# SSD stage of a two-layer hybrid model: three units of the next group's input projection among the head pairs' y products, and the older out product of the last group after its own y

## What is computed

```python
proj = u @ w_in
z = proj[..., :SSD_D_INNER]
xbc = jax.nn.silu(dwconv_centred(proj[..., SSD_D_INNER:SSD_D_INNER + SSD_CONV_DIM], conv_w, conv_b))
...
y = y_fwd + y_bwd + xh * d_skip.reshape(SSD_GROUPS, SSD_HPG)[:, :, None]
y = y.reshape(bsz, seq, SSD_D_INNER) * jax.nn.silu(z.astype(jnp.float32))
yg = y.reshape(bsz, seq, SSD_GROUPS, SSD_D_INNER // SSD_GROUPS)
yg = yg * lax.rsqrt(jnp.mean(yg * yg, axis=-1, keepdims=True) + NORM_EPS)
y = yg.reshape(bsz, seq, SSD_D_INNER) * norm_w.astype(jnp.float32)
return (y @ w_out).astype(u.dtype)
```

## Time and profile before

| | us |
|---|---|
| median of three runs | 1836.24 |
| lowest and highest run | 1832.72, 1839.12 |
| the profiled execution: its time | 1833.54 |
| the profiled execution: its span | 1831.8 |
| TensorE busy (matmuls) | 1578.1 (86%) |
| VectorE busy | 1282.2 (70%) |
| ScalarE busy | 781.0 (43%) |
| y stage of group 0, about | 149 to 183 |
| y stages of groups 1, 2 and 3 | 274 to 312, 402 to 442, 532 to 572 |
| last out products of the SSD stage | 585 to 609 |

### The profile page before, as it was taken

The page is one execution under the profiler, slowest core; times in us unless marked ns, Lnnn a source line. Parts: engine busy times, 40 slices in busy tenths (PEclk is TensorE's granted clock), DMA queues, the critical chain, the costliest instruction groups (busy, mean ns, idle before and its releaser), DMA issues.

```text
span 1831.8 us, 20798 instructions
## 1 busy us (share of the span) xinstructions
PE 1578.1 (86%) x7275; PEld 1269.4 (69%) x7275; DVE 1282.2 (70%) x1673; ACT 781.0 (43%) x1323; POOL 165.6 (9%) x200
## 2 busy tenths in 40 slices
PE   3984987987985799999998777887898999999996
PEld 1753756755754588778877556887686888888875
DVE  4577766866875676696679898997466677663355
ACT  3348465473473455513442322221234555542242
POOL 1153000000000450000001020000010000000000
PEclk7987998998997899999999986675899999999998
DMA  2233313303320523252334564662232323333231
GB/s 71 82 92 117 92 46 115 105 33 118 112 70 23 114 87 97 81 184 92 102 133 161 191 240 143 162 166 53 66 104 70 102 92 100 95 97 104 90 94 64
DMA packets 189607, 190.57 MB, mean 104 GB/s; under 512 B 47566, under 2 KB 178206, under 8 KB 185438
## 3 DMA queue, kind: packets, MB, share of 16 engines
q1 hardware_dynamic: 168926, 187.52, 32.4%
q10 hardware_dynamic: 20608, 2.10, 0.9%
HBM read 165.27 MB, written 24.31 MB: 103 GB/s over the span
## 4 chain that ended last, share of the span: by engine, by line
PE 59%; DVE 25%; ACT 9%; issue 4%; DMA 2%; ACTq 1%; SPq 1%; DVEq 0%
PE ring L1829 19%; PE ring L1830 18%; PE ring L1831 18%; ACT rows L992 3%; ACT rows L1002 3%; DVE w_lo L1224 2%; DVE rb L1631 2%; DMA rows<-log_decays 1%; DVE ul L1238 1%; PE pe_y L1972 1%; DVE cc L1348 1%; DVE s_prod L1590 1%; DVE tab L1551 1%; DVE ytmp L1502 1%; DVE rstd L1247 1%
## 5 line engine op out<-in xcount | busy, mean ns | idle before, releaser
L879 ACT ACTIVATE w_hi<-w_raw 128x1024 fp32r<-128x1024 f32 (+1 forms) x233 | 239.9, 1029 | 656.7 <-PE ring L1831 626.2
L1829 PE MATMUL ring<-uh,w_hi 128*128 128x512 f32 (+1 forms) x1160 | 461.9, 398 | 36.5 <-DVE w_lo L1224 30.1
L1830 PE MATMUL ring<-ul,w_hi 128*128 128x512 f32 (+1 forms) x1160 | 455.7, 393 | 0.0
L1831 PE MATMUL ring<-uh,w_lo 128*128 128x512 f32 (+1 forms) x1160 | 455.0, 392 | 0.0
L1224 DVE TENSOR_TENSOR w_lo<-w_raw,w_hi 128x1024 fp32r<-128x1024 f32 (+1 forms) x233 | 278.0, 1195 | 188.4 <-ACT w_hi L879 188.2
L1829 PEld LDWEIGHTS ring<-uh,w_hi 128*128 128x128 f32 (+1 forms) x1160 | 220.1, 190 | 94.7 <-DVE w_lo L1224 25.7
L1830 PEld LDWEIGHTS ring<-ul,w_hi 128*128 128x128 f32 (+1 forms) x1160 | 220.1, 190 | 47.3 <-issue 2.1
L1831 PEld LDWEIGHTS ring<-uh,w_lo 128*128 128x128 f32 (+1 forms) x1160 | 219.7, 189 | 47.4 <-issue 0.6
L1829 PE MATMUL ring<-gh,w_hi 128*128 128x512 f32 x480 | 190.5, 397 | 29.2 <-DVE w_lo L1224 16.1
L1830 PE MATMUL ring<-gl,w_hi 128*128 128x512 f32 x480 | 189.1, 394 | 0.0
L1831 PE MATMUL ring<-gh,w_lo 128*128 128x512 f32 x480 | 189.0, 394 | 0.0
(11 more groups left out here) (250 smaller groups left out, 2173.9 us busy)
## 6 DMA issues: line engine op xcount, KB each, us to landing
w_raw<-in_ffn_w_up SPq DMA_DIRECT2D x88, 512.0 KB, 3.5
w_raw<-in_ffn_w_down SPq DMA_DIRECT2D x40, 512.0 KB, 3.5
w_raw<-in_ssd_w_in SPq DMA_DIRECT2D x32, 512.0 KB, 4.4
rows<-log_decays SPq DMA_DIRECT2D x16, 1024.0 KB, 5.9
s_tables<-tab SPq DMA_DIRECT2D x16, 1024.0 KB, 6.2
slot<-s_tables SPq DMA_DIRECT2D x16, 1024.0 KB, 7.4
w_raw<-in_ssd_w_out SPq DMA_DIRECT2D x16, 512.0 KB, 3.5
w_raw<-in_ple_w_gate SPq DMA_DIRECT2D x16, 512.0 KB, 3.5
```

Of the source, the lines that this page charges most:

```text
L879: act.activation(w_hi[u % 2][:, 0:n], w_raw[:, u % 2, 0:n], ACT.Copy).then_inc(hi_done, 1)
L1829: pe.matmul(o, wh[:, k, c], rh[:, k0 + k, :], start=first and k == 0, stop=False)
L1830: pe.matmul(o, wh[:, k, c], rl[:, k0 + k, :], start=False, stop=False)
L1831: mm_ = pe.matmul(o, wl[:, k, c], rh[:, k0 + k, :], start=False, stop=last and k == nk - 1)
```

## The change

The core of the diff (the tiles `yh_last` and `yl_last` are a second pair for the last group's normed y; they lie where `xd` and `car` lay, which are done with by then):

```diff
@@ sync
-                    for n in range(GT + 2):
+                    for n in range(GT + 1):
                         row_load(n)
+                    xbc_loads(1, 2, 3)
+                    row_load(GT + 1)
                 else:
-                    xbc_loads(g, 2, 6)
+                    xbc_loads(g, 3, 6)
...
-                        for n in range(2):
-                            xbc_loads(g + 1, n, n + 1)
-                            row_load(GT * g + GT + n)
+                        xbc_loads(g + 1, 0, 1)
+                        row_load(GT * g + GT)
+                        xbc_loads(g + 1, 1, 3)
+                        row_load(GT * g + GT + 1)
@@ scalar
-                    if hp + 1 < GT and g:
-                        hi_to(w + hp + 3)
+                    if g:
+                        if hp < (GT if g + 1 < GROUPS else 2):
+                            hi_to(w + hp + 3)
+                    elif hp == 3:
+                        hi_to(w + 2)
...
-                if g < GROUPS - 1:
-                    hi_to(U[("xbc", g + 1)] + 2)
-                if g:
+                if g + 1 < GROUPS:
+                    hi_to(U[("xbc", g + 1)] + 3)
+                if 0 < g < GROUPS - 1:
                     act.wait_ge(unit_done, w + 4)
...
+                if g + 1 == GROUPS:
+                    hi_to(w + 5)
@@ vector
+                ahead = U[("xbc", g + 1)] if g + 1 < GROUPS else None
                 for hp in range(GT):
                     weigh(hp)
-                    if g:
+                    if g and hp < 2:
                         lo_to(w + hp + 2)
                     add_yoff(hp)
                     if hp:
                         finish(hp - 1)
-                    if hp + 1 < GT and g:
+                    if g and (hp < 2 or hp == 2 and ahead):
                         take_out(g - 1, hp + 1)
+                    if ahead and hp:
+                        lo_to(ahead + hp - 1)
                 finish(GT - 1)
...
                 dve.tensor_scalar(var[:], pe_s[:], 1.0 / GC, EPS, ALU.mult, ALU.add).then_inc(gvar, 1)
+                if ahead:
+                    lo_to(ahead + 3)
                 dve.wait_ge(gstd, g + 1)
                 dve.reciprocal(ytmp[:], var[:]).then_inc(grstd, 1)
                 dve.wait_ge(grstd, g + 1)
-                if g < GROUPS - 1:
-                    lo_to(U[("xbc", g + 1)] + 2)
...
+                if not ahead:
+                    take_out(g - 1, 3)
+                    lo_to(w + 4)
...
+                if not ahead:
+                    lo_to(w + 5)
@@ tensor
                 u = U[("xbc", g)]
-                for i in range(3):
-                    for kg in range(2):
-                        product(u + 2 * i + kg, T[("xbc", g)] + 2 * i, 4, 4 * kg, uh0, ul0, first=kg == 0, last=kg == 1)
-                        if g and (i, kg) == (0, 0):
-                            group_square(g - 1, GT - 1)
+                for n in range(3 if g else 0, 6):
+                    xbc_product(g, n)
...
+                def meanwhile(out, xbc):
+                    if g and out:
+                        out_product(g - 1, out)
+                    if g + 1 < GROUPS and xbc is not None:
+                        xbc_product(g + 1, xbc)
+
                 transposes(0)
                 for hp in range(GT):
-                    if hp + 1 < GT and g:
-                        out_product(g - 1, hp + 1)
+                    meanwhile(*((1, None), (2, None), (3 if g + 1 < GROUPS else None, 0), (None, 1))[hp])
                     if hp + 1 < GT:
                         transposes(hp + 1)
                     outputs(hp)
-                    if hp:
-                        group_square(g, hp - 1)
-            group_square(GROUPS - 1, GT - 1)
+                if g + 1 < GROUPS:
+                    meanwhile(None, 2)
+                    group_square(g, GT - 1)
+                else:
+                    group_square(g, GT - 1)
+                    meanwhile(3, None)
```

More of the change, by code:

```diff
@@ L178, in bidir_hybrid_kernel @@
         zs = sb("zs", [P, GT, SEQ], where=ssd)
+        last_y = ExitStack()
+        yh_last = sb("yh_last", [P, GT, SEQ], F32R, last_y)
+        yl_last = sb("yl_last", [P, GT, SEQ], F32R, last_y)
+        last_y.close()
         xd = sb("xd", [P, 2, GC], where=ssd)
@@ L198, in bidir_hybrid_kernel @@
         ssd.close()
+        YH, YL = [yh] * (GROUPS - 1) + [yh_last], [yl] * (GROUPS - 1) + [yl_last]
         def ffn_memory(layer, where):
@@ L1029, in _ @@
                     act.wait_ge(yn_done, GT * g + m + 1)
-                    act.activation(yh[:, m, :], zs[:, m, :], ACT.Copy).then_inc(yh_done, 1)
+                    act.activation(YH[g][:, m, :], zs[:, m, :], ACT.Copy).then_inc(yh_done, 1)
+                if g + 1 == GROUPS:
+                    hi_to(w + 5)
             for i in range(4):
@@ L1509, in _ @@
                                              in1=ytmp[:], op0=ALU.mult, op1=ALU.mult).then_inc(yn_done, 1)
+                if not ahead:
+                    take_out(g - 1, 3)
+                    lo_to(w + 4)
                 for m in range(GT):
                     dve.wait_ge(yh_done, GT * g + m + 1)
-                    dve.tensor_tensor(yl[:, m, :], zs[:, m, :], yh[:, m, :].bitcast(F32), ALU.subtract
+                    dve.tensor_tensor(YL[g][:, m, :], zs[:, m, :], YH[g][:, m, :].bitcast(F32), ALU.subtract
                                       ).then_inc(yl_done, 1)
+                if not ahead:
+                    lo_to(w + 5)
             for i in range(4):
@@ L1903, in out_product, with xbc_product @@
                 def out_product(g, i):
-                    product(U[("out", g)] + i, T[("out", g, i)], GT, 0, yh, yl)
+                    product(U[("out", g)] + i, T[("out", g, i)], GT, 0, YH[g], YL[g])
+                def xbc_product(g, n):
+                    product(U[("xbc", g)] + n, T[("xbc", g)] + n // 2 * 2, 4, n % 2 * 4, uh0, ul0, first=n % 2 == 0,
+                            last=n % 2 == 1)
                 u = U[("xbc", g)]
-                for i in range(3):
-                    for kg in range(2):
-                        product(u + 2 * i + kg, T[("xbc", g)] + 2 * i, 4, 4 * kg, uh0, ul0, first=kg == 0, last=kg == 1)
-                        if g and (i, kg) == (0, 0):
-                            group_square(g - 1, GT - 1)
+                for n in range(3 if g else 0, 6):
+                    xbc_product(g, n)
                 z_product(0)
```

## The result

The changed kernel is slower: 1846.44 us median of ten runs (1841.52 to 1848.56) against 1837.58 us (1832.72 to 1839.12) for ten runs of the kernel before, measured beside it. The ratio is 1.0050, with a 95% interval of 1.0039 to 1.0060. The profiled execution took 1845.06 us with a span of 1843.3 us, 11.5 more than the span of before.

What follows compares the result with a forecast made beforehand. Bounds: log decays and ScalarE's decays in the y stage, VectorE's chain to X4's split in the convolution stretch. 0.7 + 2 x (1.7 + 0.8 + 2.0) - 5.2 = +4.5 us on 1836.24 gives 1840.7; range 1831 to 1847.

Steps and rivals of the forecast that it cites:

- second rival: Stops before X0 and X4 cost full clock price, 2.1 and 2.5 us: +8.6 in all, or 1845 us; chance 0.33.
- Nothing of the three units comes off the path: Convolution stretch: X4's split keeps its place and four units still follow, so moving three units saves nothing by itself.
- Group 0: Y products at full clock bring the variance 1.3 us earlier; with X4's +2.0 the group's sum is +0.7.
- Group 3: Last group: variance 7.6 us earlier, `yl` ends 5.2 earlier, so -5.2 (bounds -4 and -7.6).
- third rival: Group 3 gains only 3 us instead of 5.2: +6.7 in all, 1843 us; its chance counted in with the second rival.
- From the variance to the convolution: VectorE's chain in groups 1 and 2: X3's rounding and split enter, other splits leave; about 0.1, taken as 0.
- X4's clock: X4 starts at half clock after some 10 us idle: +2.0 (bounds 1.4 and 2.5) in each of groups 0 to 2.
- Start of the variance: Groups 1 and 2: `weigh` slides behind the wait for X0's split, variance at 322.1 instead of 320.38: +1.7 us.
- X0's clock: Groups 1 and 2: X0 may lose clock after a 4.4 us stop; +0.8 taken, between 0 and 2.1.

Runs made afterwards that it cites:

- e3: Changed kernel with roundings and splits from X4 on one place earlier in groups 1 to 3: 1828.02 us, ratio 0.9964 to the kernel before.
- e1: Kernel before with only the last group's edits, groups 0 to 2 as before: 1829.71 us, ratio 0.9972 to the kernel before.
- e10: Changed kernel with only X3 rounded and split ahead of the variance: 1837.21 us, ratio 1.0010 to the kernel before.
- e7: Changed kernel with 14 idle matmuls between O3 and X0 in groups 1 and 2: 1845.77 us, ratio 1.0070 to the kernel before.
- e11: Changed kernel, groups 1 and 2: X0's split back behind `weigh` of head pair 2, plus 14 idle matmuls before X0: 1841.77 us, ratio 1.0047.
- e2: Changed kernel with the last group put back, only the moved units of groups 0 to 2 kept: 1850.14 us, ratio 1.0086.
- e4: Changed kernel with ScalarE rounding X0 ahead of head pair 3's decays in groups 1 and 2: 1832.91 us, ratio 0.9990 to the kernel before.
- e6: Changed kernel with 32 idle matmuls between X3 and X4 in groups 1 to 3: 1847.65 us, ratio 1.0069 to the kernel before.
- e8: Changed kernel with X0's split back behind `weigh` of head pair 2 in groups 1 and 2: 1843.16 us, ratio 1.0056 to the kernel before.
- e5: Changed kernel with both mends, the edits of e3 and of e4: 1813.32 us, ratio 0.9880 to the kernel before.

## Why the prediction was right, and where its sizes were off

The direction and most of the reasons held; the size did not. I forecast +4.5 us, and it is +9 by the medians: 1846.44 is 0.6 us inside the upper end of my range. "Slower by over 0.3%", which the ratio of 1.0050 is, had 0.36 from me, "within 0.3%" had 0.51. The second rival's +8.6 is nearer, but by luck: its prices were too high (2.1 for X0 past its slack and 2.5 for X4, where X0 lost 1.6 in all and X4 2.0), and about 4 us come from places that neither it nor my own sum had.

- **Nothing of the three units comes off the path.** Right. The transposes did not come earlier in any group, and `e3` shows that X4's split holds them: moved by one place, with those behind it, it gave 16 us.
- **Group 0.** Right: variance -1.5 (forecast -1.3), transposes +0.6 (forecast +0.7).
- **Group 3.** Right: variance -7.3 (-7.6), first own out product -5.0 (-5.2); `e1` alone is 5.1 faster in time. (My third rival's -3 lay outside the bounds of -4 and -7.6 that I gave here.)
- **From the variance to the convolution.** Right at 0 (13.5 against 13.3; my own terms add to 0.2, not 0.1), and made up as I had it: taking X3 out gave 7 us in `e10`.
- **X4's clock.** Right at +2.0: 23.9 against 21.9 us for four units, and 43.9 to 44.1 against 41.8 from the variance to the transposes.
- **Start of the variance, +1.7, and X0's clock, +0.8.** These are the two terms that were mis-sized: 3.1 us in group 2, where nothing else differs up to the variance, and 3.4 in group 1 less what O1 lost, instead of 2.5. From X0's first matmul to the variance I had 22.4 us for VectorE's chain (299.7 to 322.1) and 23.2 with the clock; it was 23.9. VectorE's chain took 23.3 (`e7`): X1's split took 2.01 us beside GpSimd's addition, and I had it at 1.1. TensorE's chain took 22.3 with X0 at full clock (`e11`) and 23.9 with X0 at 7.2 us instead of 5.6. So X0 lost 1.6, where my +0.8 past 0.4 of slack means 1.2, and the slack was gone: TensorE's chain, not VectorE's with `weigh` behind the wait, set the variance. The rule of the Trainium skill (TensorE: Matmul & The Clock Gate, section "HAM oscillation — how this bites in real kernels"), that waits between bursts put the clock back to half before each, agrees with the trace for this stop of 4.50 us: from 301.0 to 304.6 the granted clock was 0.56. It did not hold behind every shorter stop, as the last section shows.
- **What was missing.** Two places that the change does not touch and that I took as unchanged. O1 of group 1 took 7.2 us instead of 5.6, +1.6: the granted clock was 0.58 from 273.9 to 278.0, where it had been 1.00 in the kernel before; O1 of groups 2 and 3 was slow in both kernels. (So the rows of group 1 do not speak for group 2 there: before the change the y stage of group 2 began 128.0 us behind that of group 1, and only from its variance on is it 129.7.) And from the x transposes to the next y stage groups 1 and 2 took 41.0 us instead of 39.8, +1.2 each, with slower matmuls at the states; group 0 took 41 in both. Before the change and with it:

```profile
383.34 2.33 PE L1944 MATMUL ring<-xd,bseq 128*128 128x512 f32 x4 [3.13 <-DVE xd L1437]
390.08 3.68 PE L1966 MATMUL ring<-xd,bseq 128*128 128x512 f32 x4 [3.13 <-DVE xd L1450]
```

Together 4.1 us. With the 0.6 and 0.9 by which the two terms above fell short that makes up the gap of 5.2 between +4.5 and the +9.7 that the trace shows up to the first own out product; what is left is small and of both signs. In groups 1 and 2 of `e2`, `e4`, `e6`, `e7`, `e8` and `e10` it is 40.8 to 41.3 too, in `e5` 41.4 and in `e3` 42.4, and 39.7 in `e1`, so it goes with the moved units. Why the clock falls there, no run settles.

## What to carry to other kernels

Work taken from a full-looking stretch shortens it only if the stretch ends on that work: look for what starts its last uninterrupted run, here one weight split, and move that. When an early unit is put into another engine's waits, its preparation steps (round, split) must move ahead as well, or they place a wait for the slowest chain in front of work that was free. Where two chains of nearly one length run side by side, mending one shows almost nothing: count both from their common start before one is called free. Both mends together turned a loss of 0.5% into a gain of 1.2%, of which 0.3% is the last group's part.

## What was not expected of the hardware

The clock's fall did not follow the length of the last stop alone. In `e6` it was 0.57 from 348 to 352 although TensorE had stood only 1.87 us before the work went on at 347.0; in the kernel before it stayed at 1.00 through stops of 1.66 and 0.69; with 3.43 us in `e3` X4 lost nearly as much as with 9.13 in the change, and with 2.36 us in `e5` nothing. One and the same stop ended both ways: 2.52 us before O1 of group 1 was followed by 1.00 in the kernel before and by 0.58 in the change. A short stop is thus no safe one, and an edit elsewhere can move a fall to a place that it does not touch. A second number: a split took 2.01 us instead of 1.23 while GpSimd added the squares (307.57 in the change, GpSimd from 307.20 to 308.49), as the first operation of `weigh` of head pair 3 did before (1.97 instead of 1.22, at 302.71, GpSimd from 302.34 to 303.61).
